# Twelve instead of eight of the 22 steps of the FFN output products as seven block products, with the first weight sums formed in DRAM and two more ring slots

## The reference

```python
D_MODEL, SEQ, D_FF, CONV_WIDTH = 2048, 256, 5632, 3

def conv_ffn(h, w_in, conv_w, conv_b, w_out):
    s = h.shape[1]
    u = h @ w_in                                   # 256 x 2048 by 2048 x 11264
    up = jnp.pad(u, ((0, 0), (CONV_WIDTH - 1, 0), (0, 0)))
    c = conv_b
    for j in range(CONV_WIDTH):
        c = c + conv_w[j] * up[:, j:j + s]
    g, val = c[..., :D_FF], c[..., D_FF:]
    return (jax.nn.gelu(g, approximate=True) * val) @ w_out    # 256 x 5632 by 5632 x 2048

# in reference(), for each of the two layers, after the mixer:
    f = conv_ffn(rms_norm(x, ffn_norm_pre[layer]), ffn_w_in[layer], ffn_conv_w[layer],
                 ffn_conv_b[layer], ffn_w_out[layer])
    x = x + rms_norm(f, ffn_norm_post[layer])
```

## Time and profile before

| | us |
|---|---|
| median of 3 runs | 2160.96 |
| lowest, highest | 2160.62, 2161.3 |
| the profiled execution | 2161.88 |
| its span, first to last instruction | 2159.7 |
| IN0, OUT0 in it (start to end) | 337 to 855, 855 to 1084 |
| IN1, OUT1 in it | 1405 to 1923, 1923 to 2152 |

### The profile page before, as it was taken

The page is one execution under the profiler, slowest core; times in us unless marked ns, Lnnn a source line. Parts: engine busy times, 40 slices in busy tenths (PEclk is TensorE's granted clock), DMA queues, the critical chain, the costliest instruction groups (busy, mean ns, idle before and its releaser), DMA issues.

```text
span 2159.7 us, 32620 instructions
## 1 busy us (share of the span) xinstructions
PE 2147.9 (99%) x11589; PEld 1861.3 (86%) x11589; DVE 1620.6 (75%) x2280; ACT 1247.8 (58%) x1764; POOL 20.1 (1%) x40
## 2 busy tenths in 40 slices
PE   9999999999999999999999999999999999999998
PEld 8989988888888888888888889888888888888887
DVE  5667756777777777988789877567778776779787
ACT  5755755666555555655565567466665555556554
POOL 0000000000000000000000000000000000000000
PEclk9999999999999999999999999999999999999999
DMA  8566266666656566666657644666655656566575
GB/s 285 177 186 182 92 199 195 209 196 191 188 179 204 181 196 201 197 221 211 223 167 225 198 158 127 194 192 196 196 183 179 201 175 204 178 207 209 195 229 189
DMA packets 204392, 416.68 MB, mean 193 GB/s; under 512 B 13245, under 2 KB 13623, under 8 KB 203535
## 3 DMA queue, kind: packets, MB, share of 16 engines
q1 hardware_dynamic: 200687, 400.29, 58.9%
q0 software_dynamic: 3616, 15.21, 2.0%
HBM read 408.11 MB, written 7.34 MB: 192 GB/s over the span
## 4 chain that ended last, share of the span: by engine, by line
PE 97%; DVE 1%; DMA 1%; ACT 0%; issue 0%; SPq 0%; DVEq 0%; ACTq 0%
PE ps L826 29%; PE ps L780 20%; PE ps L1320 20%; PE ps L834 15%; PE ps L864 4%; PE ps L874 3%; PE ps L1563 1%; PE ps L955 1%; PE ps L1466 0%; PE ps L1085 0%; DMA w_raw<-in_ffn_w_out 0%; PE ps L927 0%; PE ps L1020 0%; PE ps L1091 0%; PE ps L1116 0%; PE ps L1028 0%
## 5 line engine op out<-in xcount | busy, mean ns | idle before, releaser
L2504 DVE TENSOR_TENSOR w_lo<-w_raw,w_hi 128x1024 fp32r<-128x1024 f32 x450 | 541.4, 1221 | 256.1 <-ACT w_hi L1783 252.3
L826 PE MATMUL ps<-xT,w_hi 128*128 128x512 f32 x2752 | 657.6, 391 | 0.0
L1783 ACT ACTIVATE w_hi<-w_raw 128x1024 fp32r<-128x1024 f32 (+1 forms) x466 | 476.8, 1040 | 228.7 <-PE ps L780 85.3
L826 PEld LDWEIGHTS ps<-xT,w_hi 128*128 128x128 f32 x2752 | 505.4, 188 | 98.2 <-issue 0.4
L834 PEld LDWEIGHTS ps<-xT,w_lo 128*128 128x128 f32 x2752 | 353.1, 191 | 13.8 <-DVE w_lo L2504 0.4
L834 PE MATMUL ps<-xT,w_lo 128*128 128x256 f32 x2752 | 358.1, 283 | 0.0
L1320 PE MATMUL ps<-w_hi,hT_hi 128*128 128x512 f32 x576 | 224.4, 390 | 0.5 <-DVE w_lo L2428 0.5
L1320 PE MATMUL ps<-w_lo,hT_hi 128*128 128x512 f32 x576 | 224.1, 389 | 0.0
L1320 PE MATMUL ps<-w_hi,hT_lo 128*128 128x512 f32 x576 | 224.1, 389 | 0.0
L780 PE MATMUL ps<-w_hi,xT 128*128 128x512 f32 x640 | 203.3, 392 | 0.0
L2428 DVE TENSOR_TENSOR w_lo<-w_raw,w_hi 128x1024 fp32r<-128x1024 f32 x126 | 151.0, 1222 | 29.4 <-ACT w_hi L1737 25.3
(11 more groups left out here) (343 smaller groups left out, 2746.0 us busy)
## 6 DMA issues: line engine op xcount, KB each, us to landing
w_raw<-in_ffn_w_in SPq DMA_DIRECT2D x352, 512.0 KB, 4.2
w_raw<-in_ffn_w_out SPq DMA_DIRECT2D x176, 512.0 KB, 4.8
w_raw<-in_shared_w_kv SPq DMA_DIRECT2D x48, 512.0 KB, 4.4
w_raw<-in_a_w_o SPq DMA_DIRECT2D x32, 512.0 KB, 4.8
w_raw<-in_b_w_in SPq DMA_DIRECT2D x32, 512.0 KB, 4.7
w_raw<-in_b_w_o SPq DMA_DIRECT2D x32, 512.0 KB, 4.3
w_raw<-in_a_w_mem_kv SPq DMA_DIRECT2D x16, 512.0 KB, 6.5
w_raw<-in_b_w_mem_kv SPq DMA_DIRECT2D x16, 512.0 KB, 4.0
```

The costliest lines, as they stand in the source:

```text
L826: mm = nc.tensor.matmul(ps[:, base + m4, :].rearrange("p (a n) -> p a n", a=2), w_hi[:, slot, cols], xT[:, :, 2 * k + c, :], start=k == c ...
L1783: nc.scalar.activation(w_hi[:, s % R, 0:width], w_raw[:, s % R, 0:width], ACT.Copy)\
L2504: nc.vector.tensor_tensor(w_lo[:, s % R, :], w_raw[:, s % R, :], w_hi[:, s % R, :].bitcast(F32), ALU.subtract)\
```

## The change

- **PAIRS 8 to 12.** In each half 12 units and 20 plain entries: 136 entries in each layer, 984 matmuls instead of 1008. LEADS is (9, 4), the lead may hold entries of the second tile, TAILS is (4, 7). Half 0 has 4 plain entries between its 12 units, half 1 has 6.
- **First sums in DRAM.** The two sums of `odd` are no longer made by DVE. During the input product POOL issues for each group of two units two copies of weight blocks from DRAM to DRAM (`odd_kept`) and, once they have landed, two transfers that add other blocks to them there (`accum_op`). These are 48 transfers of 512 KB in each layer, five in every 16 steps from the second iteration on (`beside_input`, `odd_part`). SP then loads `odd` as a `w_raw` slot of its own (512 KB), and `corner` as 256 KB, since only B22 of the right tile is still needed beside it; `left` stays 512 KB. A unit is three loads and 1.31 MB in place of two loads and 1.05 MB.
- **Forms of activations in DRAM.** Each iteration that makes forms writes them to `s_new` (one buffer), POOL sends them to `s_kept` (two transfers of 384 KB, `forms_leave`), and `sums_hi` waits for the earlier ones to have left (`s_stored`). In the output product POOL fetches the forms of each unit into one of two buffers `s_now` (384 KB, `forms_return`); the transfer for unit n is issued when unit n - 2 is done, and PE waits for `s_landed` at the `corner` entry. The forms have type float32r on both sides.
- **Deeper rings.** Where x lay there are now two more slots for `w_raw` (`x_raw`) and a sixth for `w_hi`/`w_lo` (`w6`). From entry 9 to entry 128 each ring has six slots (`turns`).
- **x returns later:** at steps 129 to 132 of 136 (`X_FREE`).

```diff
-PAIRS = 8
+PAIRS = 12
...
-LEADS = (CUT, 5)
-REST, TAILS = 3, (4, 8)
+LEADS, REST, TAILS = (CUT, 4), 3, (4, 7)
...
     def unit(half, p):
-        r = len(raws)
-        entries.extend((kind, 2 * half, p, r) for kind in ("left", "corner", "odd", "even"))
-        for tile in (2 * half, 2 * half + 1):
-            raws.append((tile, p, "unit", half * PAIRS + p))
+        e, no = len(entries), half * PAIRS + p
+        for n, kind in enumerate(("left", "corner", "odd")):
+            entries.append((kind, 2 * half, p, load(kind, 2 * half, p, e + n, no)))
+        entries.append(("even", 2 * half, p, None))
...
+SLOTS = R + 2
...
+        if 0 <= turn < wide:
+            slot = R + turn % SLOTS if turn % SLOTS < 2 else (CUT + turn % SLOTS - 2) % R
...
+        x_raw = at("x_raw", [P, 2, 1024], F32, X0)
+        w6_hi = at("w6_hi", [P, 1024], F32R, X0 + 8 * KB)
+        w6_lo = at("w6_lo", [P, 1024], F32R, X0 + 12 * KB)
...
+        s_new = at("s_new", [P, 2, 3, 2, P], F32R, KVB0)
+        s_now = at("s_now", [P, 2, 2, 3, P], F32R, KVB0)
...
             def out_weights(s_out, name, layer):
...
+                    if before is None:
+                        sp.wait_ge(x_spilled, 64 * (layer + 1))
...
+                    dst = raw_slot(r)
+                    if kind == "odd":
+                        sp.wait_ge(odd_summed, 32 * (layer * PAIRS + no // 2 + 1))
+                        src = odd_kept[layer][no].rearrange("p a n -> p (a n)")
+                    elif kind == "corner":
+                        dst, src = dst[:, 0:512], view[name][:, 2 * k + 1, 512 * (j + 1):512 * (j + 2)]
...
                 for q in range(4):
-                    pool.wait_ge(step_used, s_out + PAIR_ENDS[2 * q + 1])
+                    pool.wait_ge(step_used, s_out + X_FREE + q)
                     pool.dma_start(x[:, :, 512 * q:512 * (q + 1)],
                                    x_kept[:, :, 512 * q:512 * (q + 1)]).then_inc(x_back, 16)
+
+            def odd_part(layer, n):
+                g, part = n // 4, n % 4
+                half, p = 2 * g // PAIRS, 2 * g % PAIRS
+                chunk, tile, a, op = ((0, 0, 0, None), (1, 1, 1, None), (0, 1, 0, ALU.add),
+                                      (0, 1, 1, ALU.add))[part]
+                src = view[f"ffn_w_out{layer}"][:, 2 * p + chunk:2 * p + chunk + 3:2,
+                                                512 * (2 * half + tile):512 * (2 * half + tile + 1)]
+                dst = odd_kept[layer][2 * g:2 * g + 2, :, a, :].rearrange("u p n -> p u n")
+                if op is None:
+                    pool.dma_start(dst, src).then_inc(odd_copied, 16)
+                else:
+                    pool.wait_ge(odd_copied, 32 * (layer * PAIRS + g + 1))
+                    if part == 2 and layer + g > 0:
+                        pool.wait_ge(odd_summed, 32 * (layer * PAIRS + g))
+                    pool.dma_start(dst, src, accum_op=op).then_inc(odd_summed, 16)
+
+            def forms_leave(layer, i):
+                pool.wait_ge(s_lo, layer * (PAIRS // 2) + i + 1)
+                for b in range(2):
+                    pool.dma_start(s_kept[layer][2 * i + b], s_new[:, :, :, b, :])\
+                        .then_inc(s_stored, 16)
+
+            def beside_input(layer, s_in):
+                n = 0
+                for i in range(1, FJ):
+                    for at_step in (1, 4, 7, 10, 13):
+                        pool.wait_ge(step_used, s_in + 16 * i + at_step)
+                        if at_step == 13 and i <= PAIRS // 2:
+                            forms_leave(layer, i - 1)
+                        if n < 4 * PAIRS:
+                            odd_part(layer, n)
+                            n += 1
+                assert n == 4 * PAIRS
+
+            def forms_return(layer, s_out, no):
+                if no < 2:
+                    pool.wait_ge(s_stored, 32 + 16 * PAIRS * (layer + 1))
+                else:
+                    pool.wait_ge(step_used, s_out + UNIT_DONE[no - 2])
+                pool.dma_start(s_now[:, no % 2], s_kept[layer][no % PAIRS]).then_inc(s_landed[no % 2], 16)
...
                     if kind == "corner":
-                        return s(s4_hi, s4_lo, 0, a, 0)
+                        pe.wait_ge(s_landed[no % 2], 16 * (layer * PAIRS + no // 2 + 1))
+                        return s(2, a, 0)
...
                 def sums_hi(i):
-                    act.wait_ge(kv_spilled, 32)
-                    act.wait_ge(x_spilled, 64 * (layer + 1))
+                    act.wait_ge(s_stored, val(32 + layer * 16 * PAIRS, 32, i))
...
-                if kind == "left":
-                    outer, _, b12, _ = unit_blocks(r)
...
-                    nc.vector.tensor_tensor(
-                        out_slot(e + 2)[2].rearrange("p (a n) -> p a n", a=2), outer,
-                        b12.unsqueeze(1).to_broadcast([P, 2, 512]), ALU.add)\
-                        .then_inc(odd_sums, 1)
...
+                    nc.vector.tensor_tensor(even[:, 0:512], odd[:, 0:512], right[:, 0:512], ALU.add)\
                         .then_inc(even_sum, 1)
                     dve.wait_ge(even_sum, unit_no)
-                    nc.vector.tensor_tensor(even[:, 512:1024], even[:, 0:512], b21,
+                    nc.vector.tensor_tensor(even[:, 512:1024], even[:, 0:512], left[:, 512:1024],
                                             ALU.add).then_inc(unit_sums, 1)
```

219 lines of the change are left out of this document (113 added, 106 removed).

## The result

The changed kernel took 2171.52 us (median of 5 runs, 2170.04 to 2172.35), the kernel before 2161.3 beside it. The ratio is 1.0046, 95% interval 1.0032 to 1.0061: slower by 10 us, where 7.6 us less was forecast. The sign is wrong. That the time lies in the range (2149.5 to 2178) is luck: the range was stretched upwards for late loads and late forms in the output product, and the time was lost in the input product, where the forecast put nothing. The profiled execution took 2170.04 us.

The account below looks back on a forecast made before the run. PE's own work was taken to bound the kernel: from 2160.96 us, -10.9 for matmuls, + 2 x (1.0 + 0.5) = 3.0 for stalls and forms, + 0.3 for x, makes -7.6 and 2153.4 us; range 2149.5 to 2178.

Parts of the forecast that it names:

- What goes: Output products: four more units per half and layer save 48 matmuls at 0.2265 us, 10.9 us, the whole possible gain.
- Beside the input product: Input product: POOL's added copies, sums and forms raise the DMA share to about 0.90 and nothing waits; no cost.
- IN0 grew: Sign of being wrong: the first input product was to stay at 518 us with a DMA share near 0.9.
- sums in DRAM choke the input product: Rival, input product: waits from 5.4 us per adding transfer on; at 8.8 us the kernel takes 2312 us; chance 0.07.
- DVE in the output product: Output product: DVE alone costs nothing, but with late loads half 0 stalls 1.0 us in a layer, half 1 nothing.
- Forms come back: Output product, half 0: forms land in 5.9 us, just in time before three units; 0.5 us in a layer counted.
- x comes back late: End of the output product: returning x costs 0.3 us in layer 0 and nothing in layer 1.
- Loads in the output product land near 6 us: Expected sign in the output product: `w_raw` weight loads landing near 6 us.

Follow-up runs that it names:

- e12: The changed kernel with many odd parts moved ahead of the input products, most others at tile starts, and TAILS (2, 7) for (4, 7): 2151.01 us.
- e1: The changed kernel with the 24 adding transfers of each layer overwriting instead of adding: 2156.44 us.
- e7: e1 with a second 512 KB copy to a spare DRAM tensor beside each overwriting copy, so two copies for an add: 2173.88 us.
- e9: The changed kernel with the same transfers beside the input products, all at the end of one tile or start of the next, copies and adds alternating: 2161.38 us.
- e10: e9 with every transfer four steps later, in the middles of the tiles: 2201.16 us.
- e6: The changed kernel with TAILS (2, 7) for (4, 7), so six plain entries instead of four between half 0's units: 2166.47 us.
- e2: The changed kernel without any odd-sum transfers; the odd loads read two blocks of w_out as they are: 2160.58 us.
- e3: The changed kernel with only two of twelve forms transfers per layer leaving for DRAM, and every returning transfer reading one of these: 2174.5 us.

## Why the prediction was wrong, step by step

- **What goes, 10.9 us: right.** 48 matmuls fewer, 0.2265 us apart; e12's output products gained 10.0 of it.
- **Beside the input product: the step that failed.** It said "Then the share is about 0.90 and nothing waits". The share was right (0.88). Its parts were right too: a copy 1.6 us, as forecast, an adding transfer 3.6 where 3.2 was taken, twice a copy, as the sum of two reads had it. "Nothing waits" was wrong by 14.7 us, and IN0 grew, which the forecast had named as a sign of being wrong. The reason given, that SP has "four steps of 518/176 = 2.94 us", is a mean over the stage; the step is 2.80 us, and the loads come in clusters. In these clusters the engines stand at 0.91 and 0.93 already before the change, so the mean of unused time (197 us by the forecast, 187 with the stage's true length of 492.4) says nothing of the place where a transfer falls. It takes both, engine time and place. At the changed kernel's steps 113 us of engine time in IN0 cost 0.4 us (e1), 161 with the adding 7.85, and 154 without any adding 9.6 (e7). At the same 60 transfers IN0 is 5.7 us shorter in e9 than in the changed kernel and 10.8 longer in e10, by the place in the tile.
- **The rival "sums in DRAM choke the input product"** had the right place, and the wrong condition: from 5.4 us for an adding transfer on, that is, when the stage's total runs out. It cost 7.85 and 6.84 us at 3.6. A break-even by the total has to be replaced by one for the fullest stretch.
- **DVE in the output product: right place, too small.** In half 0 PE's weight queue waited for `w_lo` 1.4 us in OUT0 and 3.3 in OUT1 (1.0 in a layer forecast), in half 1 never, as forecast.
- **Forms come back: right place, too small.** Forecast 5.9 us to land, three short gaps in half 0, 0.5 us in a layer. The landing was 6.3 in the median, up to 8.3:

```profile
DMA to landing us min/median/max: 3.7/6.3/8.3
```

PE waited 1.4 us (two times) and 2.8 (three times), all in half 0. e6 shows the short distance between the units to be the cause: with the plain entries spread wider the waits are gone. It takes the waits for `w_lo` away as well, so it doesn't divide the loss between the two. Instead of 2 x (1.0 + 0.5) + 0.3 = 3.3 us the output products lost 10.9 - 5.0 = 5.9. This too is a low value: by the other kernels with the same order half 0 costs up to 6.2 us in a layer, against 1.5 forecast. So 1.5 was a second term that was mis-sized.
- **x comes back late: right.** Loss 0.74 us in OUT0 against 0.3. The landing's median was 6.3 as in the earlier trace rows, and DVE waited for it 5.5 us.
- **Loads in the output product land near 6 us: right,** 5.9 in the median (4.8 in the earlier trace rows), while the engines move 316 GB/s beside the units of half 0, against 209 in the earlier trace rows:

```profile
887.00:955.00 68.00, 66.52 (x292) 54.18 (x291) 66.56 (x74) 45.70 (x50) 5.84 (x11) 1.00 0.94 316
```

In the changed kernel's trace the terms of the output product were right to 2.6 us together; the term set to zero by an average was larger than the whole gain.

The Trainium skill (Collectives: The Full Stack, Part 3) prices an add in the DMA by its two reads, so at twice a copy; this case's runs agree to a tenth, 3.6 us against 1.6 for a copy and 3.3 for two.

By the Trainium skill (DMA: Bandwidth & Descriptors, Anatomy of one DMA) a transfer takes 2.0 us + bytes / 436 GB/s, an estimate of 2.9 us for the forms; the 6.3 us measured beside other loads are over twice that, and the measurement decides.

What stays open: OUT0 took 227.2 us in the changed kernel and 229.8 and 230.0 in e1 and e2, with the same order of entries. The difference lies in half 0, which lost 2.4 us there and 5.1 and 4.5 here. With one trace of each I can't say whether that is the earlier entry (by 7 us) or chance; e9 and e10, which enter it 5 us earlier and 11 later, lost 4.7 and 4.9. The median of e2 is 4.1 us above that of e1, with 48 transfers fewer in a layer, and their traces, at 2158.7 and 2158.2 us, don't show why. And e3's 3 us stay unexplained but for the hint above.

## What to carry to other kernels

Before putting transfers "beside" a stage, don't divide its idle DMA time by their cost: look at when the loads there are issued within one period of the loop. If the consumer works in bursts, the loads come in bursts too, and the room is in the stretches where the consumer does something else. Tie background transfers to those steps, one at a time, and put what is left into stages with less to load; here the places of the transfers brought 14.7 us and the wider spread of the plain entries 5, with the same instructions, and a loss of 10 us became a gain of 10.

## What the runs showed of the hardware

- A DRAM to DRAM transfer of 512 KB that adds took 3.6 us of all 16 engines and a plain one 1.6. Beside weight loads it landed in 9.1 us in the median (5.7 to 15.0), the copy in 5.8 (4.1 to 11.4). Landings of adds, changed kernel:

```profile
DMA to landing us min/median/max: 5.7/9.1/15.0
```

- It keeps POOL's queue 1.16 us to issue, a copy 0.72, and makes 128 packets more than the copy of the same bytes (20522 against 17444 for 24 of them).
- The median landing of the input products' weight loads hardly tells good from bad: 4.2 us before, 4.8 in e9, 5.0 in e10 and 5.6 in the changed kernel, though e10 is 30 us slower than the changed kernel. What differs is which loads are late.
- The mean share of the DMA engines over a stage says little of any one stretch of it: 0.62 in IN0 before, and within one iteration 0.50, 0.91, 0.50 and 0.93.
